# One core, float32 trunk of attention and retention: the low part of each weight tile, made by GpSimd, in pieces of 256 columns

## The chip, the core and the metric

The kernel runs on one core of one Trainium2 chip. The metric is the time of one execution on the device, in microseconds (us), as the median of a few runs. Engines are named as the profile names them: PE (TensorE, matmuls), PEld (its weight loads), DVE (VectorE), ACT (ScalarE), POOL (GpSimd), SP (SyncE, which issues most DMAs).

## The reference, cut to what matters

Two decoder layers of width 1024 over 512 tokens, float32. Layer 0 mixes tokens by stick-breaking attention (16 heads), layer 1 by retention (4 heads). Each is followed by a gated MLP (2816 wide, a causal convolution on its gate) and a gated embedding of a second input; an RMSNorm ends it.

```python
for i in range(DEPTH):                       # DEPTH = 2
    h = rmsnorm(x, norm_mix[i])
    m = stick_breaking_attention(h, sb_w_in[0], sb_w_out[0]) if i == 0 else \
        retention(h, ret_w_in[0], ret_w_out[0])
    x = x + m
    x = x + conv_gated_ffn(rmsnorm(x, norm_ffn[i]), ffn_w_in[i], ffn_conv_w[i], ffn_conv_b[i], ffn_w_out[i])
    x = per_layer_embed(x, p[i], norm_pl[i], pl_w_gate[i], pl_w_proj[i])
return rmsnorm(x, norm_final)
```

The change touches no formula: it is in how the weights w of every product `h @ w` are prepared.

## The kernel before, in words

**Products in three parts.** Activations lie transposed, as 8 chunks of 128 features by 512 tokens. Every factor is split into a high part (rounded to the matmul's type, names ending in h) and a low part (what is left, names ending in l), and a product is the sum of three matmuls: high by high, low by high, high by low (`three`, L324 to L335).

**Weight tiles.** The weights come as 236 tiles in a fixed order: 204 of 128 x 1024 (8 blocks of 128 columns) and 32 of 128 x 1408 (11 blocks, the output weights of the two MLPs). A tile goes through four engines:

- SP loads it into `raw`, a ring of 3 places during attention and of 2 after it (`load`, L256). It waits before each load until the low part of the tile that lay in that place is done (`w_low`, L270 and L282).
- ACT copies it into `wh`, the high part (`tile_high`, L1088; the copies are recorded on L1086), when the matmuls of an old tile have begun and the slot of `wh` and `wl` is free. This is a ring of 3 and then 4 slots. The copy adds one to `w_high`.
- POOL waits for `w_high` and writes `wl` = `raw` - `wh`, one instruction for the whole tile, which adds one to `w_low` (`split_low`, L301 to L307). POOL does nothing else.
- PE waits for `w_low` before the first matmul of the tile (`tile_ready`, L337). A tile of 1024 columns feeds 24 matmuls.

The order in each engine's queue is written out by hand. ACT makes a tile's high part some tiles ahead of PE, at places between its other work.

**Attention.** Heads go in 8 pairs, and a pair in two halves. In a half, PE makes the scores (L391 to L394, `scores`), ACT and DVE turn them into softplus values `sp`, and DVE splits these into `sph` and `spl` (`low`, L700) in the sizes 128, 256, 384 and 512 columns. PE sums them up with matmuls on L410 (`cumulate`), which wait for `sp_low`. ACT takes the exponential (L1206) and copies `ah`, DVE makes `al`, and PE multiplies by the values. Between these steps PE works on the query, key and value products of the next pair (`qkv`). Their results are scaled by DVE into `att_tmp` (L775), copied by ACT into `qh` or `k_pack`, and DVE makes the low parts of `q_pack` and `k_pack` (L700), for which the next scores wait. ACT makes one tile's high part in the first half of a pair and two in the second.

**The ends of the stages.** `x_phase` adds a product to x chunk by chunk (L734) and prepares the next norm: ACT makes `xh`, DVE makes `xl` (L720) and adds the squares into `sumsq` (L714). After the last chunk DVE splits `sumsq` (L725, L700), and PE sums it over partitions (`stats`, L355). The matmuls of the next stage begin with chunk 0 of the new x and wait for each chunk's `xl`; `stats` stands in PE's queue behind the first product or two. The start of the kernel and the end of layer 0 (`embed`) do the same in an order of their own.

The attention's output product takes 8 tiles, numbers 24 to 31. The high part of number 28 is made when the first product of this stage is done.

Of the kernel before, what the change touches and what calls it, by code (L numbers as in the profile page):

```python
# [25 lines left out]
F32 = mybir.dt.float32  # L26
F32R = mybir.dt.float32r

P = 128
# [16 lines left out]
CONV = 3  # L46
WARM_UP = 6
DMA_SCRATCH = 256


ATT_TILES = 3 * PAIRS
# [7 lines left out]
ATT_RING, RING, RAW_RING = 3, 4, 2  # L59
# [7 lines left out]
def place(n):  # L67


    if n < ATT_TILES:  # L70
        return n % ATT_RING, n % ATT_RING, W8, n // ATT_RING + 1, max(n - ATT_RING + 2, 0)
    m, left = n - ATT_TILES, n - ATT_TILES
    for tiles_, blocks_ in RUNS:
        if left < tiles_:
            break
        left -= tiles_
    free = {0: n - 1, 1: n - 1, 2: n - 2, 3: n - 2}[m] if m < RING else n - RING + 2
    return SLOTS[m % RING], m % RAW_RING, blocks_, ATT_TILES // ATT_RING + m // RAW_RING + 1, free
# [16 lines left out]
def program(nc, xT, pT, w8, w11, params, consts, outT):  # L95
    ctx = ExitStack()
    with ctx:
        def sb(name, shape, dt=F32, where=ctx):
            return where.enter_context(nc.sbuf_tensor(name, [P] + shape, dt))

        def sem(name):
            return ctx.enter_context(nc.semaphore(name))
# [5 lines left out]
        wh, wl = sb("wh", [RING, FH * P], F32R), sb("wl", [RING, FH * P], F32R)  # L108
# [70 lines left out]
        w_high, w_low, w_begun = sem("w_high"), sem("w_low"), sem("w_begun")  # L179
# [69 lines left out]
        def raw_slot(ring, r, blocks):  # L249
            wide = RAW_COLS // ring  # L250
            return raw[:, r * wide:r * wide + blocks * P]
# [47 lines left out]
        @block.gpsimd  # L299
        def _(pool):  # L300
            def split_low(n, like):  # L301

                slot, r, blocks, _, _ = place(like)
                cols = slice(0, blocks * P)
                pool.wait_ge(w_high, n + 1)
                nc.gpsimd.tensor_tensor(wl[:, slot, cols], raw_slot(ATT_RING if like < ATT_TILES else RAW_RING, r, blocks),  # L306
                                        wh[:, slot, cols].bitcast(F32), ALU.subtract).then_inc(w_low, 1)  # L307

            with pool.Fori(0, PAIRS) as i:
                for u in range(ATT_RING):  # L310
                    split_low(ATT_RING * i + u, u)
            n0 = ATT_TILES
            for tiles, _ in RUNS:
                with pool.Fori(0, tiles // RING) as i:
                    for u in range(RING):
                        split_low(n0 + RING * i + u, n0 + u)
                for n in range(n0 + tiles // RING * RING, n0 + tiles):
                    split_low(n, n)
                n0 += tiles
# [1162 lines left out]
```

## Time and profile before

| | |
|---|---|
| time, median of 3 runs | 1585.61 us (1584.87 to 1587.32) |
| span of the profiled execution, first to last instruction | 1583.1 us |
| PE busy | 1542.2 us, 97% of the span |
| DVE busy | 915.0 us, 58% |
| ACT busy | 645.1 us, 41% |
| POOL busy | 605.2 us, 38%, 236 tile instructions |

The profile gives a span for the profiled execution and no other time of it: what lies around the span is taken as the difference between the median of the runs and the span, 1585.6 - 1583.1 = 2.5 us. Times in rows are from the span's start. Matmuls overlap each other, and their ends are modelled: one of 512 columns is shown as 0.39 us while the next starts 0.23 us after it. The granted clock of TensorE is given as a share of its full 2.4 GHz.

### The profile page before, as it was taken

How to read it: one execution, taken by the hardware profiler on the slowest of the kernel's cores; microseconds unless marked ns; L12 is line 12 of the kernel's file. 1: busy time of each engine (PE TensorE's matmuls, PEld its weight loads, DVE VectorE, ACT ScalarE, POOL GpSimd, SP SyncE). 2: the span in 40 equal slices, each digit the busy share in tenths (PEclk: the TensorE clock that was granted, in tenths of full speed). 3: DMA queues.
4: the chain of work that ended last, by engine and by line, in shares of the span. 5: the costliest groups of instructions: out<-in, count | busy, mean ns of one | idle time of the engine just before them, and what ended most of it. 6: DMA issues, size and time to landing. Idle time of an engine off the chain costs nothing. (4 is left out here: it accounts for less than half of the span.)

```text
span 1583.1 us, 19904 instructions
## 1 busy us (share of the span) xinstructions
PE 1542.2 (97%) x6874; PEld 1262.7 (80%) x6874; DVE 915.0 (58%) x1217; ACT 645.1 (41%) x1027; POOL 605.2 (38%) x240
## 2 busy tenths in 40 slices
PE   8999999999999999998999999999999999999996
PEld 5777777778888888877888888888878888888874
DVE  6778787877777741158343342433677777730155
ACT  6677777433323322235353243432542332332232
POOL 3222223444444444433424334243344444444340
PEclk9999999999999999999999999999999999999998
DMA  4111201223222332223223222122222322332221
GB/s 168 42 54 40 66 13 67 77 98 103 94 93 98 103 135 92 76 81 131 81 67 101 86 80 93 66 93 93 68 92 96 103 93 93 108 123 95 86 80 54
DMA packets 37193, 137.78 MB, mean 87 GB/s; under 512 B 4128, under 2 KB 4256, under 8 KB 37024
## 3 DMA queue, kind: packets, MB, share of 16 engines
q1 hardware_dynamic: 36576, 134.61, 25.4%
q10 hardware_dynamic: 576, 2.62, 0.4%
q8 instruction: 25, 0.41, 0.1%
q14 instruction: 16, 0.13, 0.0%
HBM read 135.12 MB, written 2.10 MB: 87 GB/s over the span
## 5 line engine op out<-in xcount | busy, mean ns | idle before, releaser
L306 POOL TENSOR_TENSOR wl<-raw,wh 128x1024 fp32r<-128x1024 f32 (+1 forms) x236 | 605.0, 2568 | 943.5 <-ACT wh L1086 943.3
L331 PE MATMUL bank<-xh,wh 128*128 128x512 f32 x1280 | 504.3, 394 | 7.4 <-DVE xl L720 7.3
L334 PE MATMUL bank<-xl,wh 128*128 128x512 f32 x1280 | 500.8, 391 | 0.0
L335 PE MATMUL bank<-xh,wl 128*128 128x512 f32 x1280 | 500.1, 391 | 0.0
L1086 ACT ACTIVATE wh<-raw 128x1024 fp32r<-128x1024 f32 (+1 forms) x236 | 258.7, 1099 | 437.1 <-PE bank L331 385.9
L331 PEld LDWEIGHTS bank<-xh,wh 128*128 128x128 f32 x1280 | 241.9, 189 | 60.3 <-DVE xl L720 10.6
L335 PEld LDWEIGHTS bank<-xh,wl 128*128 128x128 f32 x1280 | 241.8, 189 | 51.0
L334 PEld LDWEIGHTS bank<-xl,wh 128*128 128x128 f32 x1280 | 241.9, 189 | 49.2 <-issue 0.2
L734 DVE TENSOR_TENSOR x<-x,bank 128x512 f32<-128x512 f32 x56 | 38.2, 682 | 234.4 <-PE bank L335 234.4
L899 DVE SCALAR_TENSOR_TENSOR conv<-gate,par,conv 128x512 f32<-128x512 f32 x88 | 150.3, 1708 | 14.7 <-DVE conv L895 6.5
L331 PE MATMUL bank<-yh,wh 128*128 128x512 f32 x352 | 136.9, 389 | 0.0
L334 PE MATMUL bank<-yl,wh 128*128 128x512 f32 x352 | 136.9, 389 | 0.0
L335 PE MATMUL bank<-yh,wl 128*128 128x512 f32 x352 | 136.9, 389 | 0.0
L700 DVE TENSOR_TENSOR yl<-yf,yh 128x512 f32 x44 | 96.1, 2183 | 41.6 <-ACT yh L1086 41.6
L1254 ACT ACTIVATE conv<-conv 128x512 f32<-128x512 f32 x44 | 27.9, 633 | 177.5 <-DVE conv L899 177.5
L331 PEld LDWEIGHTS bank<-yh,wh 128*128 128x128 f32 x352 | 66.1, 188 | 13.8
L335 PEld LDWEIGHTS bank<-yh,wl 128*128 128x128 f32 x352 | 66.1, 188 | 13.7
L334 PEld LDWEIGHTS bank<-yl,wh 128*128 128x128 f32 x352 | 66.1, 188 | 13.6
L720 DVE SCALAR_TENSOR_TENSOR xl<-x,par,xh 128x512 fp32r<-128x512 f32 x48 | 59.2, 1249 | 6.8 <-ACT xh L1086 6.8
L893 DVE TENSOR_TENSOR gate<-bank,rstd 128x512 f32<-128x512 f32 x44 | 30.4, 691 | 40.1 <-PE bank L335 35.4
L714 DVE TENSOR_TENSOR sumsq<-sumsq,square 128x512 f32<-128x512 f32 x56 | 46.7, 834 | 11.9 <-ACT square L1105 11.1
L1105 ACT ACTIVATE square<-x 128x512 f32<-128x512 f32 (+1 forms) x56 | 34.4, 620 | 39.7 <-DVE x L936 34.5
(173 smaller groups left out, 1966.9 us busy)
## 6 DMA issues: line engine op xcount, KB each, us to landing
raw<-in_w SPq DMA_DIRECT2D x204, 512.0 KB, 3.3
raw<-in_w SPq DMA_DIRECT2D x32, 704.0 KB, 4.0
x<-in_xT SPq DMA_DIRECT2D x8, 256.0 KB, 5.4
outT<-x SPq DMA_DIRECT2D x8, 256.0 KB, 2.2
pin<-in_pT ACTq DMA_DIRECT2D x2, 512.0 KB, 5.2
decay<-in_consts ACTq DMA_DIRECT2D x1, 1024.0 KB, 6.0
rotary<-in_consts ACTq DMA_DIRECT2D x1, 512.0 KB, 3.9
cst<-in_consts SPq DMA_DIRECT2D x1, 256.0 KB, 7.1
```

What stands on the lines that cost most here:

```text
L306: nc.gpsimd.tensor_tensor(wl[:, slot, cols], raw_slot(ATT_RING if like < ATT_TILES else RAW_RING, r, blocks), wh[:, slot, cols].bitcast(F3 ...
L331: first = mm(out, ah_, bh_, start=start, stop=False, skip_group_check=True)
L334: mm(out, ah_, bl_, start=False, stop=False, skip_group_check=True)
L335: return mm(out, al_, bh_, start=False, stop=stop, skip_group_check=True)
L700: vec.tensor_tensor(out, full, high.bitcast(F32), ALU.subtract).then_inc(done, 1)
L714: vec.tensor_tensor(sumsq[:], sumsq[:], square[:, par_, :], ALU.add).then_inc(sq_added, 1)
L720: vec.scalar_tensor_tensor(one(xl, k), one(x, k), col(par, g), one(xh, k).bitcast(F32), ALU.mult, ALU.subtract).then_inc(x_low, 1)
L734: vec.tensor_tensor(one(x, k), one(x, k), bank[u][:], ALU.add).then_inc(chunk_freed, 1)
L893: vec.tensor_tensor(g[:, 2:], bank[2 * u][:], rstd[:], ALU.mult).then_inc(chunk_freed, 1)
L899: vec.scalar_tensor_tensor(cv, g[:, tap:tap + T], col(par, w[tap]), cv, ALU.mult, ALU.add).then_inc(conv_step, 1)
L1086: nc.scalar.activation(out, in_, ACT.Copy, bias=0.0, scale=scale).then_inc(done, 1)
L1105: nc.scalar.activation(square[:, par_, :], one(x, k), ACT.Square).then_inc(x_squared, 1)
```

## The change

The low part of a tile is written by several instructions of at most 256 columns (`LOW_BLOCKS` = 2 blocks of 128) in place of one: four for a tile of 1024 columns, six for one of 1408 (five of 256 and one of 128). The wait on `w_high` stays ahead of the first piece, and only the last piece adds to `w_low`. Nothing changes on the other engines.

```diff
+LOW_BLOCKS = 2
...
             def split_low(n, like):
 
                 slot, r, blocks, _, _ = place(like)
-                cols = slice(0, blocks * P)
+                part = raw_slot(ATT_RING if like < ATT_TILES else RAW_RING, r, blocks)
                 pool.wait_ge(w_high, n + 1)
-                nc.gpsimd.tensor_tensor(wl[:, slot, cols], raw_slot(ATT_RING if like < ATT_TILES else RAW_RING, r, blocks),
-                                        wh[:, slot, cols].bitcast(F32), ALU.subtract).then_inc(w_low, 1)
+                for b in range(0, blocks, LOW_BLOCKS):
+                    cols = slice(b * P, min(b + LOW_BLOCKS, blocks) * P)
+                    last = nc.gpsimd.tensor_tensor(wl[:, slot, cols], part[:, cols], wh[:, slot, cols].bitcast(F32),
+                                                   ALU.subtract)
+                last.then_inc(w_low, 1)
```

POOL's queue in the attention's loop before, three tiles in one turn of the loop:

```order
8 L306 ISA
9 L306 TENSOR_TENSOR wl<-raw,wh 128x1024 [waits w_high]
10 L305 REGISTER_ALU
11 L306 TENSOR_TENSOR wl<-raw,wh 128x1024 [waits w_high]
12 L305 REGISTER_ALU
13 L306 TENSOR_TENSOR wl<-raw,wh 128x1024 [waits w_high]
14 L309 REGISTER_ALU
```

The same place in the changed kernel, where L309 is the new line of the subtraction:

```order
8 L309 ISA
9 L309 TENSOR_TENSOR wl<-raw,wh 128x256 [waits w_high]
10 L309 TENSOR_TENSOR wl<-raw,wh 128x256 x3
11 L306 REGISTER_ALU
12 L309 TENSOR_TENSOR wl<-raw,wh 128x256 [waits w_high]
13 L309 TENSOR_TENSOR wl<-raw,wh 128x256 x3
14 L306 REGISTER_ALU
```

One instruction with a wait became one with a wait and three without, with nothing between the four; between two tiles stands the same register instruction as before.

## Rows read from the trace of the kernel before

**Rows 1.** The page, busy time of each engine.

```profile
PE 1542.2 (97%) x6874; PEld 1262.7 (80%) x6874; DVE 915.0 (58%) x1217; ACT 645.1 (41%) x1027; POOL 605.2 (38%) x240
```

**Rows 2.** Waits of PE in the whole span: us in total, times, longest.

```profile
PE bank L355 <- DVE sumsq_l L700: 9.4, 4, 5.5
PE bank L331 <- DVE xl L720: 7.3, 6, 3.1
PE bank L391 <- DVE k_pack L700: 4.7, 7, 1.1
PE bank L410 <- DVE spl L700: 3.6, 8, 0.7
```

**Rows 3.** Timeline, a second half of a pair: start us, us, instruction, [idle before].

```profile
188.04 2.52 POOL L306 TENSOR_TENSOR wl<-raw,wh 128x1024 fp32r<-128x1024 f32 x1 [13.64 <-ACT wh L1086]
190.52 2.85 POOL L306 TENSOR_TENSOR wl<-raw,wh 128x1024 fp32r<-128x1024 f32 x1
188.34 2.77 DVE L700 TENSOR_TENSOR spl<-sp,sph 128x512 fp32r<-128x512 f32 x1
191.03 0.68 DVE L775 SCALAR_TENSOR_TENSOR att_tmp<-bank,rstd 128x512 f32<-128x512 f32 x1
...
193.97 0.29 DVE L700 TENSOR_TENSOR al<-sp,ah 128x128 fp32r<-128x128 f32 x1 [2.27 <-ACT ah L1086]
194.29 1.41 DVE L700 TENSOR_TENSOR k_pack<-att_tmp,k_pack 64x512 fp32r<-64x512 f32 x2
...
191.74 1.29 ACT L1086 ACTIVATE k_pack<-att_tmp 64x512 fp32r<-64x512 f32 x2 [2.83 <-DVE att_tmp L775]
```

**Rows 4.** Timeline, the attention's output product, tile 28 and its first matmul.

```profile
296.34 2.42 POOL L306 TENSOR_TENSOR wl<-raw,wh 128x1024 fp32r<-128x1024 f32 x1 [19.48 <-ACT wh L1086]
...
299.23 2.89 DVE L714 TENSOR_TENSOR sumsq<-sumsq,square 128x512 f32<-128x512 f32 x1
...
299.20 0.40 PE L331 MATMUL bank<-oh,wh 128*128 128x512 f32 x1
```

**Rows 5.** Groups of POOL by shape: count, busy us, mean ns of one, idle before.

```profile
L306 POOL TENSOR_TENSOR wl<-raw,wh 128x1024 fp32r<-128x1024 f32 x204 | 500.2, 2456 | 823.0 <-ACT wh L1086 822.9
L306 POOL TENSOR_TENSOR wl<-raw,wh 128x1408 fp32r<-128x1408 f32 x32 | 104.8, 3279 | 120.5 <-ACT wh L1086 120.5
```

**Rows 6.** Timeline of PE in the stretch of rows 3.

```profile
191.16 0.50 PE L410 MATMUL bank<-sph,negtri 128*128 128x512 f32 x1 [0.44 <-DVE spl L700]
...
195.83 0.32 PE L391 MATMUL bank<-qh,k_pack 64*128 64x128 f32 x1 [0.59 <-DVE k_pack L700]
```

**Rows 7.** Timeline, the start of the kernel.

```profile
14.98 0.50 PE L331 MATMUL bank<-xh,wh 128*128 128x512 f32 x1 [1.82 <-DVE xl L720]
...
24.44 2.73 DVE L700 TENSOR_TENSOR sumsq_l<-sumsq,sumsq_h 128x512 fp32r<-128x512 f32 x1
...
27.23 0.50 PE L355 MATMUL bank<-sumsq_h,ones_r 128*128 128x512 f32 x1 [2.19 <-DVE sumsq_l L700]
```

**Rows 8.** Timeline, from layer 0 to layer 1.

```profile
743.56 6.27 DVE L720 SCALAR_TENSOR_TENSOR xl<-x,par,xh 128x512 fp32r<-128x512 f32 x3
...
746.46 0.79 PE L331 MATMUL bank<-xh,wh 128*128 128x512 f32 x1 [3.15 <-DVE xl L720]
...
749.23 0.80 PE L331 MATMUL bank<-xh,wh 128*128 128x512 f32 x1 [1.12 <-DVE xl L720]
...
755.25 0.40 PE L355 MATMUL bank<-sumsq_h,ones_r 128*128 128x512 f32 x1
```

**Rows 9.** Windows: length, busy (count) of PE, PEld, DVE, ACT, POOL, granted clock, DMA.

```profile
66.30:97.90 31.60, 30.56 (x148) 24.52 (x149) 24.84 (x53) 23.52 (x56) 7.97 (x3) 1.00 0.15 48
97.90:131.06 33.16, 32.12 (x148) 25.96 (x149) 24.84 (x53) 23.54 (x56) 7.96 (x3) 0.95 0.15 48
743.00:753.00 10.00, 5.73 (x14) 3.84 (x13) 9.24 (x8) 4.13 (x6) 5.33 (x2) 0.66 0.71 262
```

**Rows 10.** Timeline of DVE, the last chunk of the first MLP.

```profile
684.72 2.82 DVE L720 SCALAR_TENSOR_TENSOR xl<-x,par,xh 128x512 fp32r<-128x512 f32 x1
```

## The prediction, made before the changed kernel was run

> **What bounds the kernel now.** I read the busy times first. PE is busy for 97% of the span [rows 1], so nothing but PE's idle time, and time at a lower clock, can be won. POOL is busy for 38% and bounds nothing by its own work. The second view is PE's waits [rows 2]: every large one ends with DVE, and DVE is only 58% busy. So the question is what holds DVE up at these places. The third view, the timeline, shows it. DVE's subtraction into `spl` takes 2.77 us in one place [rows 3], while one 512 wide product from a bank takes 0.68 us. It starts at 188.34, inside POOL's tile (188.04 to 190.56), and ends at 191.11, 0.55 us after POOL's end: it did not move while POOL ran. The reverse shows in POOL's next tile. It starts at 190.52, while this DVE instruction runs, and takes 2.85 us in place of 2.42 [rows 3, 4], ending 2.26 us after DVE's end. `att_tmp`, whose inputs are a bank and one SBUF tile, took 0.68 us at 191.03 with POOL at work. So a DVE instruction with two SBUF inputs and a POOL tile exclude each other, each for the whole of the other's instruction. Cutting the tile cuts how long DVE can be held.
>
> **What a piece costs.** From the two shapes, 384 columns cost 3279 - 2456 = 823 ns, 2.14 ns each [rows 5]. A tile of 1024 that meets no one takes 2.42 us [rows 4], less 1024 x 2.14 = 2.19, which leaves 0.2 us fixed. A piece of 256 is then 0.2 + 0.55 = 0.75 us, and behind another piece or behind DVE about 0.6 to 0.7, since part of the fixed time overlaps (2.26 after DVE's end against 2.42). A tile becomes 4 pieces, 3.0 us (+0.6); the 1408 one 6 pieces, +1.0. POOL's busy time goes from 605 to about 605 + 204 x 0.6 + 32 x 1.0 = 760 us, 48%, which is still no bound. No row shows two POOL instructions without a wait between them, so the fixed part could be anything from 0 (all overlapped) to 0.3 us.
>
> **How the two share.** At 190.56 POOL had its next tile ready, and DVE still went first; at 299.23 [rows 4] DVE's next instruction was issued as its last one ended, and then POOL went first (DVE took 2.89 us). I take it as strict turns: every DVE instruction with two SBUF inputs waits for at most one piece, and every piece for at most one such instruction. This limits the gain: a chain of four such instructions waits four times 0.6 us, as much as for one whole tile.
>
> **Part by part, and the sum.**
>
> *Attention's second halves, 7 of them.* Now PE waits twice, 0.44 at L410 and 0.59 at L391 [rows 6], of 8 and 7 such waits [rows 2]; with the start-up of the matmul some 1.2 us a pair. With pieces, POOL's first ends at 188.8 and `spl` at 189.35 in place of 191.11, so the wait at L410 (needed at 190.7) goes: 0.5. What is late next is `k_pack`. `att_tmp` ends at 190.0, ACT copies until 191.3 (1.29 us [rows 3]), its exponentials and `ah` take 0.9 more, so `al` is asked for at 192.25 in place of 193.97. There POOL is still at its second tile: `al` and the two `k_pack` instructions wait for a piece each, 192.7 + 0.2 + (0.6 + 0.55) x 2 = 195.2 in place of 195.70. PE comes 0.5 earlier and still waits there. Gain 0.5 a pair, 3.5 in all. Ends: nothing (every turn costs 0.15 more) and 1.2 a pair, 8.4 in all (no wait left).
>
> *The start.* `xl` of chunk 5 holds PE for 1.82 us [rows 7], behind tile 1; with pieces it ends 1.3 us earlier. Behind it, `sumsq` of chunk 5 waits out tile 2 and `sumsq_l` tile 3 (2.73 us [rows 7]). Tile 1 then lets `sumsq` begin 0.3 earlier, the `sumsq` of chunk 5 waits 0.5 in place of 1.75, the two behind it and the copy 0.3 to 0.6 each (+1.5), and `sumsq_l`, behind a piece of tile 3, 0.5 in place of 2.0: -0.3 - 1.25 + 1.5 - 1.5 is 1.5 less. Tile 3 also begins 1 us sooner relative to it, so that less of it lies in this chain: `sumsq_l` ends at 24.7 in place of 27.17. PE's L355, now at 27.23, comes 2.5 earlier. Against it, tile 0 comes later and shifts the first `xl` by 0.3, which is in this. Ends 1 and 3.5.
>
> *From layer 0 to layer 1.* Three `xl` take 6.27 us here because two tiles hold the first two [rows 8], and PE loses 3.15 + 1.12 us, and more because its granted clock is 0.66 over 743 to 753 [rows 9] after the idle time. With pieces they end at 744.8, 745.9 and 747.1 in place of 746.41, 749.17 and 749.83. What is late next is `sumsq_l`: with two `sumsq` and a copy it has turns with the second tile and ends at 747.1 + 3 x (0.6 + 0.55) + 0.9 = 751.4. L355, which stands at 755.25 now, could start then. I take 3.0 of these 3.8 us, since a dip of the clock, which I expect to stay, can bring PE there 0.8 later. Ends 1.7 (the first wait alone) and 5.
>
> *Tile 28.* This is the cost. PE needs it at 299.20 and POOL ends it at 298.76 [rows 4]: 0.4 us of slack. With pieces it takes 0.6 more, and three DVE instructions (two `xl`, one `sumsq`) get turns of 0.55 in between, so that it ends near 300.6: 1.4 us lost. Ends 0.2 and 1.9.
>
> *Other ends of stages.* At the two other waits before L355 [rows 2], and where PE waits for `proj` behind each of the MLPs, the chain is `xl` (2.82 us [rows 10]), `sumsq`, its copy, `sumsq_l`: four turns in place of one long wait. I get 0.1 to 0.3 us at each of the four, 0.9 together (at rows 10: 2.3 us of waiting before, now 0.6 + 0.6 + 0.3 + 0.5 = 2.0). Ends -1 and 5.
>
> *What is hidden.* PE waits for no tile at all in the waits [rows 2]. Beyond the first tiles the ring holds two tiles or more in front of PE, 24 matmuls of 0.23 us each, 11 us in all. SP's loads wait for `w_low` and so start 0.6 to 2 us later, and ACT's high part and PE behind them draw on the same reserve. In the MLPs DVE gets through its blocked instructions sooner, which brings nothing: PE does not wait there. The last 5.5 us wait for `sumsq_l` [rows 2] has no tile beside it and stays.
>
> Sum: -3.5 - 2.5 - 3.0 + 1.4 - 0.9 = -8.5 us. Against the profiled span, 1583.1 - 8.5 = 1574.6, and with the 2.5 us outside it (the median of the runs less the span) 1577.1, which is 0.54% under the median of 1585.6.
>
> The clock adds a spread on either side. The pair from 97.90 took 33.16 us at a mean granted clock of 0.95 and its neighbour 31.60 at 1.00 [rows 9]: a dip to 1.2 GHz costs 1.6 us, and 3 of the 8 pairs have one, after PE's short idle times and small matmuls. I count these as unchanged; none left would give 4.8, two more would cost 3.2.
>
> A rule weighed against the trace: the fixed cost. Rows 4 and 5 give 0.2 us for each extra instruction. The Trainium skill, "GPSIMD Engine Reference", section "Performance versus the Vector engine", has 4497 ns for a two-input float32 instruction of 2048 columns; set against the 2.42 us of 1024 here this leaves about 0.3 us fixed, an estimate from that page, by which each turn is 0.1 longer and the sum would be about -5.
>
> **Rivals.**
>
> *A: POOL keeps its way through the four pieces.* In the trace a wait instruction stood between two tiles where DVE got in; between pieces there is none. Then DVE is held for 3.0 us in place of 2.4. Each place where it holds PE costs 0.6 more: 7 pairs (4.0), four ends (2.3), two tiles at 743 (1.1), three in the start (1.7), tile 28 0.2: +9.3, 1594.9 us. It decides as soon as DVE's `spl` beside a tile reads 3.3 us and not 1.3. Against it: at 190.56 the wait had long been met and DVE still went first [rows 3]. The Trainium skill, "GPSIMD Engine Reference", section "Instruction dispatch", says that a POOL core starts the next instruction when its own share is done, without waiting for the others, which would favour this rival; no row before the change can show it. 11%.
>
> *B: turns eat the gain.* If a piece costs 0.9 us and not 0.75, and every turn with it 0.15 more, the pairs gain nothing, the ends of stages lose 1, the start and 743 gain 1 and 1.7, tile 28 costs 1.9: between -2 and +1, some 1585 us. For it: the chains of `sumsq`. Against it: the rows' 0.2 us. 14%.
>
> *C: no wait is left in the pairs*, the clock holds, and the upper ends add up: -8.4 - 3 - 4 + 1 - 1 - 3 = -18, 1567 us. For it, DVE is only 58% busy. 10%.
>
> **How the numbers follow.** My forecast has 65%: 1577 us. About 0.2%, 3.2 us, is what a measurement of this kernel can tell from no change. Faster by more than that takes in the forecast and C, less 0.01 for its upper end: 0.74. Within it lie B and that end: 0.15. Slower is A: 0.11. The range leaves out A and the far half of C: 1569 to 1585.
>
> **What would show it.** In the changed profile `spl` beside a tile near 1.3 us, a piece near 0.7 to 0.75, POOL near 760 us busy; no wait at L410, a shorter one at L391; L355 of the start near 24.8; a wait for `wl` (tile 28) of about 1.4 us near 297; PE's `xl` waits at 743 down to some 2.3 together. The forecast is wrong if DVE's blocked instructions grow with the tile (A), if a piece is near 0.9 (B), or if the dips of the clock change in number.

## The result, and the profile after

The changed kernel took 1575.66 us (median of 17 runs, 1571.26 to 1591.27), the kernel before, on the same chip, 1585.13 us (17 runs, 1582.51 to 1587.66). The ratio is 0.9948, with the interval 0.9933 to 0.9964: faster by 0.52%. The profiled execution has a span of 1573.9 us, against 1583.1 before. The forecast was 1577.0 in a range of 1569 to 1585. Three of the 17 runs of the changed kernel, 1585.8 to 1591.3 us, lie above that range; the last section comes back to them.

Busy times of the changed kernel, from the page (columns as in rows 1):

```profile
PE 1536.6 (98%) x6874; PEld 1258.3 (80%) x6874; DVE 771.5 (49%) x1217; ACT 650.2 (41%) x1027; POOL 813.2 (52%) x1012
```

DVE executes the same 1217 instructions as in [rows 1] and is busy for 143 us less, since what the trace counts as busy held the time a blocked instruction waits. POOL gained 208 us, part of it real (four starts for one) and part the same kind of waiting, now on its side. The groups of POOL by shape (count, busy us, mean ns, idle before):

```profile
L309 POOL TENSOR_TENSOR wl<-raw,wh 128x256 fp32r<-128x256 f32 x976 | 799.5, 851 | 727.6 <-ACT wh L1090 727.3
L309 POOL TENSOR_TENSOR wl<-raw,wh 128x128 fp32r<-128x128 f32 x32 | 14.7, 459 | 0.0
```

PE's waits over the whole span (total us, times, longest), to set beside [rows 2]:

```profile
PE bank L359 <- DVE sumsq_l L704: 10.1, 5, 5.5
PE bank L395 <- DVE k_pack L704: 5.5, 6, 1.1
PE bank L335 <- DVE xl L724: 4.2, 9, 1.4
PE bank L335 <- DVE proj L925: 2.9, 2, 1.5
PE bank L335 <- POOL wl L309: 2.9, 2, 1.5
```

The 3.6 us for `spl` are gone, `xl` fell from 7.3 to 4.2. `k_pack` rose from 4.7 to 5.5, and a releaser that was absent before is there: POOL's `wl`, with one wait of 1.47 us in the start (the matmul at 23.79) and one of 1.43 us for tile 28.

The second half of a pair, the place of [rows 3] and [rows 6]. The timeline of POOL, DVE and PE (start, us, instruction, idle before and releaser); the first row is all eight pieces of two tiles:

```profile
181.10 6.68 POOL L309 TENSOR_TENSOR wl<-raw,wh 128x256 fp32r<-128x256 f32 x8 [13.17 <-ACT wh L1090]
181.40 1.12 DVE L704 TENSOR_TENSOR spl<-sp,sph 128x512 fp32r<-128x512 f32 x1
182.44 0.68 DVE L779 SCALAR_TENSOR_TENSOR att_tmp<-bank,rstd 128x512 f32<-128x512 f32 x1
...
183.63 0.40 PE L414 MATMUL bank<-sph,negtri 128*128 128x512 f32 x1
...
185.39 0.66 DVE L704 TENSOR_TENSOR al<-sp,ah 128x128 fp32r<-128x128 f32 x1 [2.26 <-ACT ah L1090]
186.08 2.25 DVE L704 TENSOR_TENSOR k_pack<-att_tmp,k_pack 64x512 fp32r<-64x512 f32 x2
...
188.47 0.32 PE L395 MATMUL bank<-qh,k_pack 64*128 64x128 f32 x1 [0.88 <-DVE k_pack L704]
```

`spl` starts 0.30 us into POOL's first piece and takes 1.12 us, not 2.77: it waits until that piece is over, then goes, although POOL's next piece needed no semaphore. PE reaches its 512 wide matmul at L414 (L410 before) with no idle time. The price shows further down: `k_pack` comes while POOL is still at work and takes 2.25 us, not 1.41, since each of its two instructions waits a piece. PE waits 0.88 us for it, more than the 0.59 of [rows 6].

Tile 28, the place of [rows 4]:

```profile
290.13 0.47 PE L335 MATMUL bank<-oh,wh 128*128 128x512 f32 x1 [1.43 <-POOL wl L309]
```

From layer 0 to layer 1, the place of [rows 8]:

```profile
737.67 3.51 DVE L724 SCALAR_TENSOR_TENSOR xl<-x,par,xh 128x512 fp32r<-128x512 f32 x3
738.96 0.50 PE L335 MATMUL bank<-xh,wh 128*128 128x512 f32 x1 [0.69 <-DVE xl L724]
...
745.55 0.50 PE L359 MATMUL bank<-sumsq_h,ones_r 128*128 128x512 f32 x1 [0.62 <-DVE sumsq_l L704]
```

Three `xl` took 6.27 us and take 3.51.

The windows of two pairs and of this stretch (columns as in rows 9):

```profile
124.60:155.76 31.16, 30.28 (x148) 24.45 (x149) 24.42 (x53) 23.56 (x55) 9.76 (x12) 1.00 0.14 50
155.76:188.47 32.71, 31.83 (x149) 25.87 (x149) 24.42 (x53) 23.55 (x55) 9.75 (x12) 0.95 0.14 48
738.00:748.00 10.00, 8.34 (x38) 5.91 (x37) 7.59 (x8) 4.88 (x8) 8.09 (x8) 1.00 0.66 228
```

**The account.** To see where the 9.2 us of the span came from, I took the same matmul in both traces at the end of each stretch and subtracted the start times. The difference of one stretch is what that stretch won or lost. The stats matmul is PE's first matmul on `sumsq_h` (L355 before, L359 after), which ends a stage:

| Stretch | Change, us | Forecast |
|---|---|---|
| Start, to the stats matmul (27.23 to 25.12) | -2.1 | -2.5 |
| Second halves, 7 of them | -3.0 | -3.5 |
| First half of the first pair, and the last of attention | -1.2 | 0 |
| Tile 28 (299.20 to 290.13) | +1.6 | +1.4 |
| Output product, tile 28 to the stats matmul (328.40 to 322.04) | +2.7 | -0.25 |
| Layer 0 to 1 (755.25 to 745.55) | -4.7 | -3.0 |
| The three other ends of stages | -1.4 | -0.65 |
| Slow stretches of the clock (1.2 GHz): three fewer in attention, two new ones later | -1.1 | 0 |
| Sum | -9.2 | -8.5 |

The pieces of the clock are what is left once the idle time of PE is compared: -4.4 in attention, +1.6 at 322, +1.6 at 1145. The slow stretch at 746 before, which is gone too, is inside the row of layer 0 to 1. One row of the table has the wrong sign, the output product, and several of the runs below are aimed at it.

### The profile page after: what moved, and what is told of

Same layout as the page of the kernel before. It is cut to its first block, busy times and chain, and to the rows that moved or that the text cites. A ratio compares the mean times of both kernels' runs of the same rounds, so it can differ in the third digit from the quotient of the medians.

```text
span 1573.9 us, 20676 instructions
## 1 busy us (share of the span) xinstructions
PE 1536.6 (98%) x6874; PEld 1258.3 (80%) x6874; DVE 771.5 (49%) x1217; ACT 650.2 (41%) x1027; POOL 813.2 (52%) x1012
## 4 chain that ended last, share of the span: by engine, by line
PE 77%; issue 14%; POOL 6%; DVE 2%; ACT 0%; DMA 0%; POOLq 0%; DVEq 0%; SPq 0%; ACTq 0%
PE bank L335 23%; PE bank L338 23%; PE bank L339 23%; POOL wl L309 6%; PE bank L601 2%; PE bank L596 2%; PE bank L600 2%; DVE sumsq L718 0%; DVE xl L724 0%; PE bank L660 0%; DVE x L1083 0%; DMA raw<-in_w 0%; DVE sumsq_l L704 0%; DVE x L940 0%; DVE gated L937 0%
## 5 line engine op out<-in xcount | busy, mean ns | idle before, releaser
L309 POOL TENSOR_TENSOR wl<-raw,wh 128x256 fp32r<-128x256 f32 x1008 | 813.0, 838 | 727.6 <-ACT wh L1090 727.3
L903 DVE SCALAR_TENSOR_TENSOR conv<-gate,par,conv 128x512 f32<-128x512 f32 x88 | 91.4, 1038 | 14.7 <-DVE conv L899 6.5
L906 DVE TENSOR_TENSOR up<-bank,rstd 128x512 f32<-128x512 f32 x44 | 30.4, 692 | 70.0 <-PE bank L339 70.0
L704 DVE TENSOR_TENSOR yl<-yf,yh 128x512 f32 x44 | 41.6, 946 | 40.1 <-ACT yh L1090 40.1
L718 DVE TENSOR_TENSOR sumsq<-sumsq,square 128x512 f32<-128x512 f32 x56 | 52.7, 941 | 11.9 <-ACT square L1109 11.1
L724 DVE SCALAR_TENSOR_TENSOR xl<-x,par,xh 128x512 fp32r<-128x512 f32 x48 | 41.4, 878 | 20.2 <-ACT xh L1090 20.1
```

The lines of the kernel that those rows point to most:

```text
L309: last = nc.gpsimd.tensor_tensor(wl[:, slot, cols], part[:, cols], wh[:, slot, cols].bitcast(F32), ALU.subtract)
L704: vec.tensor_tensor(out, full, high.bitcast(F32), ALU.subtract).then_inc(done, 1)
L718: vec.tensor_tensor(sumsq[:], sumsq[:], square[:, par_, :], ALU.add).then_inc(sq_added, 1)
L724: vec.scalar_tensor_tensor(one(xl, k), one(x, k), col(par, g), one(xh, k).bitcast(F32), ALU.mult, ALU.subtract).then_inc(x_low, 1)
L903: vec.scalar_tensor_tensor(cv, g[:, tap:tap + T], col(par, w[tap]), cv, ALU.mult, ALU.add).then_inc(conv_step, 1)
```

## The experiments

### Size of the piece, in both directions

```diff
-LOW_BLOCKS = 2
+LOW_BLOCKS = 4
```

> Pieces of 512 columns: 2 for a tile of 1024, 3 for one of 1408. A piece alone should read about 0.2 + 512 x 2.14 ns = 1.3 us, POOL's busy time about 605 + 204 x 0.2 + 32 x 0.4 = 660 us plus its turns. Theory (DVE and POOL take strict turns, the piece is what DVE waits for): in the attention's second halves the subtraction into spl beside a tile reads up to 1.9 us, the wait at the cumulate matmuls stays away, and the wait for k_pack before the next scores stays between 0.5 and 1.0, so the pairs keep their gain of 0.4 us each. Tile 28 is late by only 0.2 + 0.55 - 0.4 = 0.4 to 0.9 us where the changed kernel loses 1.6. The end of the attention's output product loses about half of what it loses with 256. Time 1574 to 1579. Rival (the gain comes from how long DVE is held, in proportion): half of the 9.5 us is lost, 1580.

1578.62 us (1577.36 to 1579.92), ratio 0.9958 (0.9944 to 0.9972). POOL's piece of 512 reads 1438 ns in the mean, its busy time 699.8 us. The time lies in the range expected, but the interval reaches the rival's 1580 too, so that the time does not decide. The trace fits the theory: `spl` beside a tile took 1.66 us, and PE still waits for `k_pack` (0.86 us a pair). The pairs kept 0.45 us each, the start won nothing, PE did not wait for tile 28, the output product after it cost 0.2, and layer 0 to 1 won only 1.25.

```diff
-LOW_BLOCKS = 2
+LOW_BLOCKS = 1
```

> Pieces of 128 columns: 8 for a tile of 1024, 11 for one of 1408. A piece alone should read about 0.46 us as the 128 column rests of the changed kernel do, a tile 3.4 to 3.8 us. Theory (turns): the wait for k_pack in the second halves falls from 0.9 to under 0.3, since three turns of 0.35 us take the place of three of 0.6, 4 to 5 us won over the pairs; tile 28 and the loads behind it are later still, 2.5 to 4 us lost against the changed kernel at the attention's output product. Time 1572 to 1580. Rival (the fixed cost of a piece and the later low parts decide): slower than the changed kernel by 4 us or more, over 1580.

1561.26 us (1560.88 to 1566.33), ratio 0.9859 (0.9837 to 0.9880): 10.7 us below the range that was expected, so the expectation was wrong in size and the rival in sign. The groups of POOL in this kernel:

```profile
L309 POOL TENSOR_TENSOR wl<-raw,wh 128x128 fp32r<-128x128 f32 x1984 | 983.2, 532 | 543.6 <-ACT wh L1090 543.3
```

The second half of a pair with pieces of 128, same place as above:

```profile
176.14 7.21 POOL L309 TENSOR_TENSOR wl<-raw,wh 128x128 fp32r<-128x128 f32 x13 [10.41 <-ACT wh L1090]
176.44 0.83 DVE L704 TENSOR_TENSOR spl<-sp,sph 128x512 fp32r<-128x512 f32 x1
...
180.14 0.55 DVE L704 TENSOR_TENSOR al<-sp,ah 128x128 fp32r<-128x128 f32 x1 [2.27 <-ACT ah L1090]
180.72 1.71 DVE L704 TENSOR_TENSOR k_pack<-att_tmp,k_pack 64x512 fp32r<-64x512 f32 x2
```

`spl` takes 0.83 us and `k_pack` 1.71. No wait for `k_pack` is left in PE's waits, and a pair is 1.38 us shorter than before. The account by the same matmuls splits the 14.8 us between the two profiled spans (1573.9 and 1559.1): the second halves give 6.8 (7 x 0.95), the ends of stages 4.3 (layer 0 to 1 1.6, the two MLPs 1.1 each, the retention 0.5), three slow stretches of the clock fewer 4.7, and the output product 0.6. (The slow stretch behind the start is the only one in this trace apart from the end's.) Tile 28 takes back 1.2 and the start 0.6, so that tile 28 and the output product together lost 0.6 us against the changed kernel, not the 2.5 to 4 expected. What grew is PE's wait for `wl`, 6.4 us in all, 2.32 at tile 28.

The smallest piece, half of that:

```diff
-                for b in range(0, blocks, LOW_BLOCKS):
-                    cols = slice(b * P, min(b + LOW_BLOCKS, blocks) * P)
+                for at in range(0, blocks * P, P // 2):
+                    cols = slice(at, at + P // 2)
```

> Pieces of 64 columns: 16 for a tile of 1024, 22 for one of 1408. By the fixed 0.18 to 0.2 us a piece reads about 0.32 us and a tile 4.7 us (start to start 0.28 to 0.3 us), 6.5 us for the large one, where PE takes 5.5 and 7.6 us for the matmuls of one. With the turns POOL is busy nearly all the time in the MLPs and falls behind where DVE has many instructions with two SBUF inputs. Theory: POOL's busy time near 1200 us, waits for wl appear in the MLPs and the kernel is slower than pieces of 128, 1565 to 1650. Rival (smaller is still better, as from 256 to 128): under 1561.

1579.6 us (1577.2 to 1583.9), ratio 0.9966 (0.9952 to 0.9981). The time lies in the range expected, though not by the way expected: no wait for `wl` appears in the MLPs. The pairs keep their 1.38, but POOL is busy for 83% (1319 us, where 1200 were expected), and PE waits for `wl` in the start (5.2 us) and at tile 28 (3.4), and for `xl` at the end of the output product (4.8) and of the retention (5.2):

```profile
PE 1541.4 (98%) x6874; PEld 1262.8 (80%) x6874; DVE 751.2 (48%) x1217; ACT 645.5 (41%) x1027; POOL 1318.6 (83%) x3972
```

```profile
PE bank L335 <- DVE xl L724: 11.1, 3, 5.2
PE bank L335 <- POOL wl L309: 8.6, 2, 5.2
```

Tile 28 costs 3.6 us, the output product 4.9 more. A part of this is not POOL's fixed time. Here DVE does not get its turn each time. The last `xl` of the output product asks at 321.36, while POOL is at work, and takes 3.43 us, where it takes 0.75 alone:

```profile
315.92 11.80 POOL L309 TENSOR_TENSOR wl<-raw,wh 128x64 fp32r<-128x64 f32 x33
321.36 3.43 DVE L724 SCALAR_TENSOR_TENSOR xl<-x,par,xh 128x512 fp32r<-128x512 f32 x1 [3.84 <-ACT xh L1090]
```

Nine more pieces started at their undisturbed distance of 0.28 us before DVE got in. Eleven DVE instructions of this run were held like this, for 1.0 to 3.9 us, while 4 to 14 pieces passed; each of them had asked just as POOL went from one tile to the next. In the kernels with pieces of 512, 256 and 128 no DVE instruction was held for longer than one piece (1.11, 0.60 and 0.36 us at most). So of the sizes tried 128 columns is the best in this kernel. Towards larger pieces it is a DVE instruction's wait that costs; towards 64 columns POOL's fixed time, which is paid once per piece, and these long waits. How much each of the two takes was not separated.

### Which stages the gain and the loss come from

The output product's tiles 24 to 35 whole, all else in pieces of 256:

```diff
+PEELED_WHOLE = 36
...
-                for b in range(0, blocks, LOW_BLOCKS):
-                    cols = slice(b * P, min(b + LOW_BLOCKS, blocks) * P)
+                step = blocks if whole else LOW_BLOCKS
+                for b in range(0, blocks, step):
+                    cols = slice(b * P, min(b + step, blocks) * P)
```

> As the changed kernel, but tiles 24 to 35 (the attention's output product and the four behind it) are each made by one instruction as before. Theory: the wait of PE for tile 28 (1.6 us in the ledger of the changed kernel) and the 2.6 us at the first L359 behind it go, since both come from low parts that are later, the first directly, the second through the loads into raw that wait for w_low and the high parts behind them in ACT's queue. The other steps stay. 4 us under the changed kernel, 1571 to 1573. Rival (the loss at the first L359 is the turns of xl, sumsq and sumsq_l alone): tile 28 gives 1.6 and the rest stays only if the last tiles are in pieces, which they are not here, so this run does not tell it apart; the timeline of ACT's waits for loads does.

1574.3 us (1570.62 to 1584.11, 10 runs), ratio 0.9939 (0.9920 to 0.9958). Both losses are gone: the steps of the account at tile 28 and in the output product are 0.0, layer 0 to 1 stays at -4.65, and the profiled span is 1571.8. That the losses came from these twelve tiles is shown. The median, 1574.3, missed the 1571 to 1573 expected: with these tiles whole, 0.9 us won at the end of attention and 0.4 in the seventh second half are lost again, and the clock differs between runs (below).

The reverse, pieces in the 24 tiles of attention alone:

```diff
-                for b in range(0, blocks, LOW_BLOCKS):
-                    cols = slice(b * P, min(b + LOW_BLOCKS, blocks) * P)
+                step = LOW_BLOCKS if like < ATT_TILES else blocks
+                for b in range(0, blocks, step):
+                    cols = slice(b * P, min(b + step, blocks) * P)
```

> Pieces of 256 columns only for tiles 0 to 23, all others in one instruction. Theory: the start gives 2.1 us and the pairs 0.4 each, with 0.9 at their end 6 us; the output product costs nothing, the 4.7 us between the layers are not won. Without the dips of the clock 1579; each dip more or less in the pairs moves it by 1.6, so 1575 to 1580. Rival (the gain is mostly between the layers): 1581 or more.

1579.78 us (1576.66 to 1585.47, 10 runs), ratio 0.9964 (0.9952 to 0.9976). The start gave 2.0, six of the seven second halves 0.42 each, the output product nothing, layer 0 to 1 only 0.3. The time is at the upper end of the range expected. The 0.9 expected at the end of attention did not come, since tiles 24 and up are whole there. So attention's share of the gain and that of the first product of layer 1 are separate.

### The cause of the loss in the output product

Two causes were open. The first: DVE's `sumsq` chain, four instructions with two SBUF inputs or a cast, gets four turns with POOL's last tiles. The second: SP's loads. The raw weights have a ring of few slots, and a slot is free only when `w_low` says that POOL has read it; each tile's load then starts late, ACT's high part waits for it, and the activations of the last chunks are behind that high part in ACT's queue. ACT's waits in the 30 us of the output product say which it might be. Before (299 to 328):

```profile
ACT wh L1086 <- DMA raw<-in_w: 9.5, 4, 3.6
```

and of the changed kernel (290 to 322):

```profile
ACT wh L1090 <- DMA raw<-in_w: 16.7, 5, 6.1
```

Its timeline on ACT shows the queue: each `xh` stands right behind a `wh` that waited for its load. The order was the same before, but there the last of these high parts waited for PE and not for its load:

```profile
322.03 1.06 ACT L1086 ACTIVATE wh<-raw 128x1024 fp32r<-128x1024 f32 x1 [2.21 <-PE bank L331]
323.00 0.71 ACT L1086 ACTIVATE xh<-x,par 128x512 fp32r<-128x512 f32 x1
```

And of the changed kernel:

```profile
312.04 1.06 ACT L1090 ACTIVATE wh<-raw 128x1024 fp32r<-128x1024 f32 x1 [2.90 <-DMA raw<-in_w]
...
316.39 1.06 ACT L1090 ACTIVATE wh<-raw 128x1024 fp32r<-128x1024 f32 x1 [2.15 <-DMA raw<-in_w]
317.36 0.70 ACT L1090 ACTIVATE xh<-x,par 128x512 fp32r<-128x512 f32 x1
```

DVE's last `xl` followed at 318.09, after 2.45 us of idle time for this `xh`, and PE's stats matmul at 322.04 waited 2.18 us for `sumsq_l`:

```profile
318.09 0.75 DVE L724 SCALAR_TENSOR_TENSOR xl<-x,par,xh 128x512 fp32r<-128x512 f32 x1 [2.45 <-ACT xh L1090]
...
320.89 1.09 DVE L704 TENSOR_TENSOR sumsq_l<-sumsq,sumsq_h 128x512 fp32r<-128x512 f32 x1
```

Before, the same chain was

```profile
323.74 2.82 DVE L720 SCALAR_TENSOR_TENSOR xl<-x,par,xh 128x512 fp32r<-128x512 f32 x1
...
327.66 0.69 DVE L700 TENSOR_TENSOR sumsq_l<-sumsq,sumsq_h 128x512 fp32r<-128x512 f32 x1
```

From the last `xl` to the end of `sumsq_l` it took 4.6 us before and takes 3.9 now, so its turns do not make it longer. But it begins 27.96 us after the first matmul of tile 28 (290.13), where it began 24.54 us after it (299.20). 3.4 later less 0.7 shorter is the +2.7 of the account.

The first test moves ACT's activation ahead of the high part and leaves the code of POOL and SP as it is:

```diff
-                tile_high(N_ATTOUT + RING + m)
+                if m < RING:
+                    tile_high(N_ATTOUT + RING + m)
...
+                if m >= RING:
+                    tile_high(N_ATTOUT + RING + m)
```

> The changed kernel (pieces of 256) with one thing moved in ACT's queue: in the attention's output product ACT makes the high part of x's chunks 4 to 7 before the high parts of tiles 32 to 35, not behind them. Theory (the 2.6 us lost at the first L359 come from ACT waiting there for loads into raw, which started late since w_low was late, with xh of the last chunks queued behind): the wait of PE for xl (1.4 us) and for sumsq_l (2.2 us) go from 3.5 to under 1 us, so the step at the first L359 is at least 2.5 us better, and the kernel 1572 to 1574. Tile 28 stays late by 1.6. Rival (the turns of xl, sumsq and sumsq_l with the pieces of the last tile): no more than 0.5 us better, 1575 or more.

The row that decides, in its trace:

```profile
333.85 0.50 PE L359 MATMUL bank<-sumsq_h,ones_r 128*128 128x512 f32 x1 [0.80 <-DVE sumsq_l L704]
```

The wait fell from 2.18 to 0.80 us. From the first matmul of tile 28, at 304.95 here, to this one are 28.9 us, against 31.9 in the changed kernel (290.13 to 322.04) and 29.2 before (299.20 to 328.40). The loss is gone, and tile 28's 1.6 stays, while ACT's high parts still wait 14.3 us for their loads: late loads cost nothing once no `xh` stands behind them. The last tile's pieces begin 27.6 us after tile 28's first matmul, as in the changed kernel (27.4), but the chain now runs ahead of most of them, so this run alone does not exclude the turns. The time of the run, 1577.95 us (1571.16 to 1591.49, 10 runs), ratio 0.9956 (0.9926 to 0.9987), missed the 1572 to 1574 expected and does not show it: five runs lie at 1571.2 to 1573.3 and five at 1582.6 to 1591.5, which is the clock's doing (below).

The second test goes at POOL: tiles 24 to 31 whole and 32 to 35, the last ones, in pieces, so that the loads come in time but DVE's chain still has its turns.

```diff
-PEELED_WHOLE = 36
+PEELED_WHOLE = 32
```

> Pieces of 256, but tiles 24 to 31 whole; tiles 32 to 35, the ones whose low parts meet the end of the first x_phase, are in pieces, which the run before had whole too. Theory (late loads): tiles 32 and 33 are loaded on time again, so most of the 2.6 us comes back, and the step at the first L359 lies between -0.5 and +1 us against the kernel before. Tile 28 gives its 1.6 us back. Rival (turns at the end of the phase): the step stays at +2.6.

```profile
336.61 0.50 PE L364 MATMUL bank<-sumsq_h,ones_r 128*128 128x512 f32 x1 [0.89 <-DVE sumsq_l L709]
```

The step of the output product is -0.3 us, not +2.7. Turns with the last tiles cost nothing, they won the 0.3 that the prediction had. ACT's waits for loads in this stretch (300 to 337) are back at 9.9 us. 1573.57 us (1569.98 to 1586.99, 10 runs), ratio 0.9930 (0.9909 to 0.9952). The rival of the turns falls, the late loads stand. More slots for the raw tiles would test the same from a third side; this was not tried.

### Two versions that beat both kernels

Pieces of 128 with tiles 24 to 35 whole (`LOW_BLOCKS = 1`, `PEELED_WHOLE = 36`):

> Pieces of 128 columns everywhere but for tiles 24 to 35, which are whole. With pieces of 128 alone PE waited 2.3 us for tile 28 and 3.0 at the first L359; the kernel before waited 0 and 0.9. Theory: 4 us under pieces of 128 alone, 1557 to 1558. If the gain of the small pieces is in the clock alone, it stays at 1561.

1558.78 us (1558.42 to 1560.26), ratio 0.9832 (0.9818 to 0.9845). This is 0.8 above the range expected. The steps at tile 28 and in the output product are 0.0, the ends of the two MLPs and of the retention give 1.4 each and layer 0 to 1 gives 6.2. Against pieces of 128 everywhere the time alone does not show a gain, since the intervals overlap (0.9837 to 0.9880 there); the account does, with 4.0 us won at these two steps and 1.35 lost in the seventh second half. A window of 34.15 us, somewhat longer than a pair:

```profile
65.20:99.35 34.15, 34.15 (x171) 27.90 (x171) 27.99 (x62) 27.17 (x65) 12.93 (x25) 1.00 0.18 62
```

PE has no idle time in it, and the clock is whole. What was left was a wait for `wl` of up to 2.7 us at the start, where nothing is ahead of the first tiles. The last version gives these three tiles pieces of their own sizes, and leaves the rest:

```diff
+START_STEPS = (8, 2, 4)
...
-            with pool.Fori(0, PAIRS) as i:
+            for n, step in enumerate(START_STEPS):
+                split_low(n, n, step=step)
+            with pool.Fori(1, PAIRS) as i:
```

> Pieces of 128 with tiles 24 to 35 whole, and at the start tile 0 whole, tile 1 in pieces of 256, tile 2 in pieces of 512. With pieces of 128 PE waits there 0.8, 1.0 and 2.2 us for the tiles themselves. Theory: 0.5 to 1.5 us better than without, 1557 to 1558.5; the first matmul of the first norm's sum near 24.8 where pieces of 256 have 25.1 and pieces of 128 have 25.4 to 25.9. Rival (the start is bound by the chain of sumsq, not by the tiles): no difference, 1558.8.

1558.01 us (1557.46 to 1559.07), ratio 0.9825 (0.9811 to 0.9838). The waits for `wl` in the start fell from 3.6 us to 0.3, but a wait of 2.0 us for `sumsq_l` took their place. The stats matmul comes at 25.35 us, where it came at 25.45 without the sizes of their own and 24.8 was expected, and the two profiled spans differ by 0.1 us. The two intervals overlap too. So this last step is not shown to be a gain, and the rival, that the start is bound by the chain of `sumsq`, stands. Either is some 17 us better than the changed kernel.

### Is it DVE's turns in the pair?

With pieces of 256 as in the changed kernel, ACT makes the high part of the second tile of each second half behind the exponentials, so that POOL's pieces of that tile come after `k_pack`:

```diff
+                for tile in late:
+                    tile_high(*tile)
...
-                slot(p, 1, par_, tiles=[(n + 6, i, step), (n + 7, i, step)])
+                slot(p, 1, par_, tiles=[(n + 6, i, step)], late=[(n + 7, i, step)])
```

> The changed kernel (pieces of 256) with the high part of the second tile of each second half made by ACT behind the exponentials and not ahead of them, so that POOL's last four pieces no longer lie across al and k_pack. Theory: PE's wait for k_pack (0.88 us, 7 times) goes, 0.9 us a pair or 6 us; and since PE no longer idles in the pairs, the half-speed stretches of the clock go from the pairs too, in the profiled execution and in all others, so that the times lie within about 3 us of each other as with pieces of 128, 1566 to 1570, where the changed kernel has some executions at 1586 and more. Rival (the dips come from the matmuls on few rows in scores and values, not from the idle time): 6 us better in the best executions, but single ones still 10 us above.

1567.88 us (1564.6 to 1570.21), ratio 0.9879 (0.9864 to 0.9894). The time is in the range expected. In its timeline `k_pack` is back at its undisturbed time, and so is the `al` in front of it (0.29 us in place of 0.66):

```profile
182.83 1.41 DVE L704 TENSOR_TENSOR k_pack<-att_tmp,k_pack 64x512 fp32r<-64x512 f32 x2
```

and one pair's window has no idle time of PE and a whole clock:

```profile
94.04:124.24 30.20, 30.20 (x149) 24.45 (x148) 23.83 (x54) 23.60 (x56) 9.50 (x12) 1.00 0.15 53
```

Each second half is 1.38 us shorter than before, as with pieces of 128. ACT's freed time is not what won it: from the start of `att_tmp` to the start of `al` it is 2.94 us here (179.57 to 182.51) and 2.95 in the changed kernel (182.44 to 185.39). So the wait that was left in the pairs of the changed kernel was the turns of `al` and the two of `k_pack`: either shorter turns or no turns take it away, and both end at the same 1.38. One part of the expectation failed. The times were to lie within 3 us of each other and spread by 5.6; none of the four was above 1570.3, though.

## Why the prediction was right, and where it was not

The time, 1575.66 us, lies 1.3 us below the forecast, and the mechanism is the forecast's. That the number is so close is partly luck. The output product came out 2.9 us worse than forecast, and the start, the second halves and tile 28 1.1 worse together; layer 0 to 1, the other ends, the stretches of attention counted at nothing, and the clock came out 4.7 better together. On balance this is 0.7 of the 1.3. The rest is what lies around the span: 1.8 us in the profiled run (1575.66 - 1573.9), not the 2.5 that the forecast took from the median and the span of different runs. The runs of the changed kernel alone spread by 20 us.

- **A piece and a turn.** Forecast: a piece 0.75 us, 0.6 to 0.7 behind another, 1.3 us for `spl` beside a tile, POOL at 760. Measured: a piece alone 0.74 us, start to start 0.695 at 256 columns and 0.42 at 128, from which come 2.15 ns a column and 0.145 us fixed; `spl` 1.12; POOL 813, since its pieces wait for DVE too, and the trace counts that as busy. From the figure of the Trainium skill, "GPSIMD Engine Reference", section "Performance versus the Vector engine", the prediction had an estimate of 0.3 us for the fixed part; the traces have half of it, so the smaller estimate held.
- **Strict turns.** Right for the change: `spl` fell with the piece, 2.77, 1.12, 0.83 us at 1024, 256 and 128 columns. Rival A, that POOL keeps its way, wanted 3.3 and is refuted at 256 columns. It is not refuted as a rule: at 64 columns POOL kept its way in eleven places, for up to 3.9 us. The Trainium skill, "SBUF — State Buffer", section "SBUF: two separate sides", describes an exclusive lock on the port pair which the first to start holds for a whole instruction; the trace agrees (1.12 - 0.69 = 0.43 us of waiting, less than one piece). The prediction has this for instructions with two SBUF inputs; the cast into `sumsq_h`, which has one, waited too (0.43 us alone, 0.83 beside pieces of 256). The rule in the Trainium skill, "GPSIMD Engine Reference", section "Instruction dispatch", by which a core goes on to the next instruction without waiting for the others, did not decide here at 256 columns: no DVE instruction was held for more than 0.60 us. The runs do not show whether it is behind the long waits at 64.
- **Second halves.** -3.5 forecast, -3.0 measured. The wait at L414 (L410 before) went, and `k_pack` became the late one with two turns, both as written. The sign named for it, a shorter wait at L391, failed: the wait at L395 (L391 before) is longer, 0.88 us against 0.59, because PE comes there earlier; the pair gains all the same.
- **The start.** -2.5 against -2.1, with L359 at 25.12 (24.8 forecast). The 1.47 us that PE waits there for `wl` were not in the forecast.
- **Layer 0 to 1.** -3.0 forecast, -4.7 measured. 0.8 of the difference was set aside for a dip of the clock that I expected to stay: the clock read 0.66 over those 10 us [rows 9] and reads 1.00 now. The chain from the three `xl` to the end of `sumsq_l` took 7.83 us, as forecast (7.84), but it began 0.9 us sooner, measured from the first stats matmul ahead of it (695.76 before, 690.73 after), which I had not counted. My range of 1.7 to 5 held it.
- **Tile 28.** +1.4 forecast, +1.6 measured, a wait of 1.43 us for `wl`, at 290.13 and not near 297, since what lies ahead of it had won 10.7 us.
- **Other ends.** -0.65 forecast for three of them, -1.4 measured.
- **The failed step** is in "What is hidden": "SP's loads wait for `w_low` and so start 0.6 to 2 us later, and ACT's high part and PE behind them draw on the same reserve". In most stages this held. In attention's output product it did not: there PE was covered, but ACT's queue was not, because the activations of the last chunks stand in it behind a high part that waits for its load. "Other ends of stages" counted -0.25 at this end and it cost +2.7. The runs with the activation moved ahead and with the tiles whole both show it. The lateness was mis-sized as well: counted from tile 28's first matmul, SP's loads began 2.8 to 4.6 us later than before (the third and the ones behind it; 7.61 to 10.41 us for the third), not 0.6 to 2: a tile's four pieces with DVE's turns between them took up to 4.3 us there, where a whole tile that meets no one takes 2.4. I had asked whether PE waits for a tile, and not who stands behind the tile's high part on ACT.
- **The clock.** "I count these as unchanged": net -1.1 us in this profile, between +3 and -5 as allowed. The prediction counts three dips in the pairs; the trace before has four in attention, since the first pair has one too (granted clock 0.95 over 33.8 to 66.3). That whole runs would differ by up to 20 us in the clock was not foreseen.

## What to carry to other kernels

Where two engines share a port for a whole instruction, the length of the one that is not urgent is a cost of the one that is: cut it, and measure the size in both directions, for the best one here (128 columns, 1558 us with the exceptions) was half of the change's, and at 64 columns the turns themselves were no longer kept each time. Exempt the stages in which the cut instruction is itself what others wait for, as where a ring of few slots feeds the next load (PE waited 2.3 us for tile 28 with pieces of 128, and not at all with it whole); exempting the start brought nothing that could be measured. Before calling a later load covered, follow it past PE: to the queue of the engine that takes the load in, and to what stands behind it there.

## What the runs showed of the hardware

**Who gets the port.** Down to 128 columns DVE and POOL took strict turns, at 64 they did not always: the longest wait of a DVE instruction was 1.11, 0.60, 0.36 and 3.9 us with pieces of 512, 256, 128 and 64 columns. Why is open.

**The clock can fall into step with a loop.** With pieces of 256, PE idles 0.88 us in a pair of 31.16 us, once each time. The changed kernel and its near versions then have spread or split times: 14 of the 17 runs of the changed kernel lie at 1571.3 to 1579.8 us at a granted clock of 0.990 to 0.994, and three at 1585.8, 1589.4 and 1591.3 at 0.984, 0.983 and 0.980. In a profile of the upper kind (the run with tiles 32 to 35 in pieces) two pairs in a row read

```profile
65.20:99.35 34.15, 33.26 (x149) 26.84 (x148) 24.35 (x53) 23.54 (x56) 9.76 (x12) 0.90 0.14 44
99.35:133.50 34.15, 33.26 (x149) 26.74 (x149) 24.32 (x53) 23.54 (x56) 9.77 (x12) 0.90 0.15 49
```

Each pair is 3.0 us longer at 0.90: a slow stretch at 1.2 GHz, of the same length in every pair from the second on to the seventh. In the profiles in which PE waits for nothing in the middle pairs (pieces of 128, or the tile made late) none of these pairs had one; the first pair did in some. The times of those kernels never split, but only the two best versions are close together (1.6 and 1.8 us over five runs each); pieces of 128 and the late tile spread by 5.5 and 5.6.

Idle time alone does not explain it. The kernel before idles longer in a pair, 0.44 and 0.59 us [rows 6], has short slow stretches in some pairs (0.95 in the window from 97.90 [rows 9]), and its 17 runs lie within 2.7 us of their median. With pieces of 512 PE idles 0.86 us in a pair, and the five runs lie within 2.6 us. What makes a run fall into the upper kind was not tried, and stays open.

**The cost of a fine cut is a busy figure, not a time, until a point.** POOL's busy time went 605, 700, 813, 984, 1319 us from whole tiles to 64 columns. Up to 984 the kernel got faster; at 1319 it was back at 1579.6, in part through the long waits at 64 columns.
